# Context's post norm, next norm, keys and values beside the latents' network, and weight splits first in the context's steps

## What is computed

```python
for i in range(DEPTH):                      # DEPTH = 2
    sh1, sc1, gt1, sh2, sc2, gt2 = ada_mods(c, w_ada[i], b_ada[i])
    csh1, csc1, cgt1, csh2, csc2, cgt2 = ada_mods(c_ctx, w_ada[i], b_ada[i])
    h_lat = modulate(rms_norm(x, g_mix_pre[i]), sh1, sc1)
    h_ctx = modulate(rms_norm(ctx, g_mix_pre[i]), csh1, csc1)
    # i = 0: y = pool_mixer(h);  i = 1: y_lat = attention of x over keys of ctx and x
    x = x + gt1 * rms_norm(y_lat, g_mix_post[i])
    m_lat = sq_relu_mlp(modulate(rms_norm(x, g_mlp_pre[i]), sh2, sc2), w_mlp_in[i], w_mlp_out[i])
    x = x + gt2 * rms_norm(m_lat, g_mlp_post[i])
    if i == 0:                              # the same for ctx, with csh, csc, cgt
        ctx = ctx + cgt2 * rms_norm(m_ctx, g_mlp_post[i])
```

## Time and profile before

| | before |
|---|---|
| median of 3 runs | 3835.47 us (3830.47 to 3838.3) |
| profiled execution | 3837.7 us |
| its span | 3835.9 us |
| PE busy | 3651.2 us, 95% |
| DVE busy | 2173.2 us, 57% |
| ACT busy | 1311.9 us, 34% |
| POOL busy | 268.9 us, 7% |

### The profile page before, as it was taken

The page is one execution under the profiler, slowest core; times in us unless marked ns, Lnnn a source line. Parts: engine busy times, 40 slices in busy tenths (PEclk is TensorE's granted clock), DMA queues, the critical chain, the costliest instruction groups (busy, mean ns, idle before and its releaser), DMA issues.

```text
span 3835.9 us, 45608 instructions
## 1 busy us (share of the span) xinstructions
PE 3651.2 (95%) x18034; PEld 2952.3 (77%) x18034; DVE 2173.2 (57%) x3522; ACT 1311.9 (34%) x1876; POOL 268.9 (7%) x362
## 2 busy tenths in 40 slices
PE   6999999999999999999999999998899968999997
PEld 5888956788888888964789878888688746587886
DVE  6555544646545555644676768766655555544444
ACT  3222443233222322344224323444322235533221
POOL 0000122001000000113001010020000010200000
PEclk9999999999999999989999999999999968999998
DMA  5444201334442443310343343334333311012220
GB/s 230 180 159 161 101 23 53 135 129 166 163 165 110 170 165 139 122 71 1 107 176 121 136 161 148 137 122 165 121 147 134 137 50 44 1 45 88 99 98 34
DMA packets 84228, 451.94 MB, mean 118 GB/s; under 512 B 10192, under 2 KB 10640, under 8 KB 47152
## 3 DMA queue, kind: packets, MB, share of 16 engines
q1 hardware_dynamic: 81936, 439.35, 31.0%
q0 software_dynamic: 2080, 9.67, 0.7%
HBM read 446.88 MB, written 2.10 MB: 117 GB/s over the span
## 4 chain that ended last, share of the span: by engine, by line
PE 87%; DVE 5%; issue 3%; ACT 3%; POOL 1%; DMA 0%; DVEq 0%; SPq 0%; POOLq 0%; ACTq 0%
PE ps L607 22%; PE ps L606 22%; PE ps L608 22%; PE ps L1486 3%; PE ps L1522 2%; PE ps L2781 1%; PE ps L980 1%; PE ps L982 1%; PE ps L1504 1%; PE ps L981 1%; PE ps L1226 1%; PE ps L2195 1%; ACT WH L513 1%; PE ps L2196 1%; PE ps L2197 1%
## 5 line engine op out<-in xcount | busy, mean ns | idle before, releaser
L606 PE MATMUL ps<-nH,WH 128*128 128x512 f32 x2416 | 955.1, 395 | 7.1 <-DVE nL L738 7.1
L607 PE MATMUL ps<-nL,WH 128*128 128x512 f32 x2416 | 951.9, 394 | 0.0
L608 PE MATMUL ps<-nH,WL 128*128 128x512 f32 x2416 | 951.1, 394 | 0.0
L524 DVE TENSOR_TENSOR WL<-raw,WH 128x2048 fp32r<-128x2048 f32 (+2 forms) x308 | 673.6, 2191 | 483.2 <-ACT WH L513 482.3
L513 ACT ACTIVATE WH<-raw 128x2048 fp32r<-128x2048 f32 (+2 forms) x308 | 560.4, 1824 | 619.0 <-PE ps L608 579.2
L606 PEld LDWEIGHTS ps<-nH,WH 128*128 128x128 f32 x2416 | 457.3, 189 | 118.2 <-ACT nH L722 9.4
L607 PEld LDWEIGHTS ps<-nL,WH 128*128 128x128 f32 x2416 | 457.1, 189 | 101.7 <-issue 2.2
L608 PEld LDWEIGHTS ps<-nH,WL 128*128 128x128 f32 x2416 | 456.8, 189 | 98.4
L606 PE MATMUL ps<-hH,WH 128*128 128x512 f32 x1072 | 422.5, 394 | 2.2 <-DVE h L1193 2.2
L607 PE MATMUL ps<-hL,WH 128*128 128x512 f32 x1072 | 423.2, 395 | 0.0
L608 PE MATMUL ps<-hH,WL 128*128 128x512 f32 x1072 | 422.2, 394 | 0.0
(11 more groups left out here) (395 smaller groups left out, 5344.0 us busy)
## 6 DMA issues: line engine op xcount, KB each, us to landing
raw<-in_wst SPq DMA_DIRECT2D x282, 1024.0 KB, 4.8
araw<-in_ast SPq DMA_DIRECT2D x225, 512.0 KB, 5.7
raw<-in_wst SPq DMA_DIRECT2D x18, 512.0 KB, 3.4
row<-in_ast SPq DMA_DIRECT2D x15, 512.0 KB, 15.0
cw<-in_cw POOLq DMA_DIRECT2D x4, 1024.0 KB, 6.0
h<-in_xT SPq DMA_DIRECT2D x1, 2048.0 KB, 8.4
raw<-in_wst SPq DMA_DIRECT2D x8, 256.0 KB, 2.6
out<-h SPq DMA_DIRECT2D x8, 256.0 KB, 2.0
```

The source lines that it names most:

```text
L524: dve.q.tensor_tensor(M.WL[k % NW][:, 0:n], M.raw[k % NR][:, 0:n], M.WH[k % NW][:, 0:n].bitcast(F32), ALU.subtract).then_inc(*v_wlo.up(k))
L606: pe.q.matmul(to, hi[:, i, cc], xh, start=i == 0, stop=False)
L607: pe.q.matmul(to, hi[:, i, cc], xl, start=False, stop=False)
L608: t = pe.q.matmul(to, lo[:, i, cc], xh, start=False, stop=i == nk - 1)
```

## The change

- In `context_on_act` and `context_on_dve` the `yield` moves: a step does the weight split, then lets the latents' step run, and only then its own hidden layer.
- `latents_*` has 31 steps instead of 34. The sum of the first norms comes at step 3, the pools at 10, 12, 14, 16; DVE applies the pooling mean one step ahead of ACT's `gH`, and `scr` is used with four tiles instead of two where the input of the pool is made.
- The context's post norm leaves `context_on_*`. Together with the next norm, keys and values it forms `tail_*`, which runs step by step beside the latents' network from its first step. The key's two weight slots stand in the plan behind the network's seventeenth and eighteenth.
- Modulation rows: two instead of one in every other slot of the latents' network, none in the key's slots.
- The context's keys and the latents' keys go to `cB`, which must wait for the last modulation row; scratch tiles move; `narrow`, which takes two of the eight banks away, comes behind the projections of the attention; a wait of the `ma` copies for the context is dropped.

```diff
-POOLED_STEPS = (11, 13, 15, 17)
-RENEWED = {22: (0, 1), 23: (2,), 24: (3, 4), 25: (5,), 26: (6, 7)}
-LATENTS_STEPS = 34
+POOLED_STEPS = (10, 12, 14, 16)
+RENEWED = {19: (0, 1), 20: (2,), 21: (3, 4), 22: (5,), 23: (6, 7)}
+LATENTS_STEPS = 31
+
+KEYS_STEP = 16
...
-    cols("w_qkv_2", (0,), 0, KT, 1024, 512, 256)
+    for n in range(2):
+        out.insert(SHARED[1] + KEYS_STEP + 1 + 2 * n, ("w_qkv_2", (0,), 0, KT, 1024 + 256 * n, 256))
...
+        if a[:5] == "w_mlp" and k % 2 == 0:
+            more = 2
...
-        if SHARED[0] <= k < SHARED[1]:
+        if SHARED[0] <= k < SHARED[1] or a == "w_qkv_2":
...
+    key.scr = [M.cB[1][:, i * C:i * C + C] for i in range(4)]
+    key.qx, key.ssq = key.scr[1:3], (key.scr[0], key.scr[3])
+    key.rs = key.small
+    key.srs = key.small[:, :].rearrange("p (a b) -> p a b", a=2)
...
-            lat.vT = sb(sc, "vT", [128, S])
+            lat.vT = [sb(sc, f"vT{i}", [128, S]) for i in range(2)]
...
-        def mlp2_dve(dve, g, p, l, q, was, free):
-
-            into = into_ma(p, M.ma)(g)
-
-            def sink(dve, ci, o):
-                if ci == 0:
-                    dve.wait_ge(*free(o))
-                into(dve, ci, o)
-
-            yield from ffn_dve(dve, g, p, NF2, False, M.hH2, M.hL2, sink)
+        def mlp2_dve(dve, g, p, l, q, was):
+            yield from ffn_dve(dve, g, p, NF2, False, M.hH2, M.hL2, into_ma(p, M.ma)(g))
...
             for ci in range(CHUNKS2):
                 for f in (0, 2):
                     step_dve(dve)
+                    yield
                     hidden(ci, f)
-                    yield
                 for _ in range(2 if ci else 0):
                     step_dve(dve)
                     yield
             for _ in range(2):
                 step_dve(dve)
                 yield
-            yield from post_dve(dve, g + "post", con, lambda i: M.mac[:, i, :], lambda i: a_ev.to(g, "acc", i // 2),
-                                V("g_mlp_post_2", 0), mod(2, 0, 5, 1), v_mod.to(2, 0, 5, 1), x_after(con, "ctxpoolpost"))
...
+        FIRST = ((0, 1, 2), (3, 4), (5, 6), (7,))
+
         def latents_pe(pe):
             for s in range(LATENTS_STEPS):
-                if s == 4:
+                if s == 3:
                     b, free = take(FIN, "sum")
                     pe.wait_ge(*free)
                     pe.wait_ge(*v_ssum.to(FIN, 7))
@@ -2362,25 +2353,24 @@
                         pe.q.matmul(b[:, 4 + j:5 + j], M.fin[2][:, c], M.ones[:, 0:1], start=True, stop=False)
                         t = pe.q.matmul(b[:, 4 + j:5 + j], lat.scr[2][:, c], M.epsc[:, 0:1], start=False, stop=True)
                     t.then_inc(*mm.up(FIN, "sum"))
-                if s == 5:
+                if s == 4:
+                    spread_pe(pe, POOL2, M.fin[3])
...
-                if s == 20:
+                if s == 17:
                     sum_pe(pe, POST2, M.fin[2])
-                if s == 21:
+                if s == 18:
                     spread_pe(pe, POST2, lat.scr[3])
-                if s == 27:
+                if s == 24:
                     put_back(POST2, "rstd")
-                if s == 28:
                     sum_pe(pe, MLP2, M.fin[2])
-                if s == 29:
+                if s == 25:
...
-                if s in (6, 7):
+                if s in (5, 6):
                     dve.wait_ge(*mm.to(POOL2, "rstd"))
-                    for i in range(4 * s - 24, 4 * s - 20):
-                        if i >= 2:
-                            dve.wait_ge(*a_xhi.to(POOL2, i - 2))
+                    dve.wait_ge(*mm.to(FIN, "rstd"))
+                    for i in range(4 * s - 20, 4 * s - 16):
+                        if i >= 4:
+                            dve.wait_ge(*a_xhi.to(POOL2, i - 4))
                         ev = empties(v_xr, POOL2, "rstd") if i == 7 else v_xr.up(POOL2, i)
-                        dve.q.tensor_tensor(lat.scr[i % 2][:, :], h_tile(i), bank(POOL2, "rstd")[:, :], ALU.mult).then_inc(*ev)
+                        dve.q.tensor_tensor(lat.scr[i % 4][:, :], h_tile(i), bank(POOL2, "rstd")[:, :], ALU.mult).then_inc(*ev)
                         if i == 7:
                             v_xr.again(POOL2, 7)
-                if 8 <= s < 16:
-                    f = s - 8
+                if 7 <= s < 15:
+                    f = s - 7
...
+                                  v_ylo.to(POOL2, f - 2) if f >= 2 else a_xhi.to(POOL2, 4 + f))
+                if 8 <= s < 16:
+                    pool_low_dve(dve, POOL2, s - 8, M.gH, M.gL, lat.scr[s % 2][:, :])
+                if s - 1 in POOLED_STEPS:
+                    for i in (s - 11, s - 10):
                         add(POST2, i, M.fin[2], odd)
-                if s == 20:
+                if s == 18:
                     inverse(POST2)
...
-                if s >= 30:
+                if 26 <= s < 30:
                     dve.wait_ge(*mm.to(MLP2, "rstd"))
-                    for i in (2 * s - 60, 2 * s - 59):
+                    for i in (2 * s - 52, 2 * s - 51):
                         times2_dve(dve, i)
-                        if i:
-                            low2_dve(dve, i - 1)
-                if s == LATENTS_STEPS - 1:
+                        if i >= 2:
+                            low2_dve(dve, i - 2)
+                if s == 30:
+                    low2_dve(dve, 6)
...
+        def tail_pe(pe):
             g, p = "ctxkey", key
+            yield from norm_pe(pe, "ctxmlppost", p)
             yield from norm_pe(pe, g, p)
             xs, ready = normed_x(p, g)
             slot_pair(pe, "w_qkv_2", C, xs, ready, [("kc0", "raw"), ("kc1", "raw")])
             yield
             slot_pair(pe, "w_qkv_2", C, xs, ready, [(g, "v", i) for i in range(2)])
-            values_pe(pe, g, p)
             yield
             for name in ("kc0", "kc1"):
                 head_pe(pe, p, name)
+            yield
+            values_pe(pe, g, p)
+            yield
+            yield
             for name in ("kc0", "kc1"):
                 head_spread_pe(pe, p, name)
...
+        def tail_dve(dve):
             g, p = "ctxkey", key
+            yield from post_dve(dve, "ctxmlppost", p, lambda i: M.mac[:, i, :], lambda i: a_ev.to("ctxmlp", "acc", i // 2),
+                                V("g_mlp_post_2", 0), mod(2, 0, 5, 1), v_mod.to(2, 0, 5, 1), x_after(con, "ctxpoolpost"))
             gain_dve(dve, g, V("g_mix_pre_2", 8), 2, 1, 0, 1)
-            dve.wait_ge(*mm.to("latmlp0", "o", last_chunk(NF2), 7))
             yield from norm_dve(dve, g, p, x_tile(con), x_after(con, "ctxmlppost"), ())
             step_dve(dve)
             yield
             step_dve(dve)
+            yield
+            yield
+            yield
             values_dve(dve, g, p, 0)
-            yield
             for name in ("kc0", "kc1"):
                 head_root_dve(dve, p, name)
+            yield
+            yield
+            dve.wait_ge(*v_row.to(8 * len(adas) - 1))
             for i, name in enumerate(("kc0", "kc1")):
                 head_out_dve(dve, p, name, key_dst(p, i), False)
...
-            now.extra = narrow()
-            weave(latents_on_pe(pe), keys_pe(pe), beside_latents)
+            weave(latents_on_pe(pe), tail_pe(pe), beside_context)
```

More of the change, by code:

```diff
@@ L332, in memory @@
             M.hL2 = sb(sc, "hL2", [128, 2, 4, S], F32R)
[L333 to L344, removed]
-    cx.close()
+            key.small = sb(sc, "smallk", [128, 16])
+            with ExitStack() as one:
+                M.mac = sb(one, "mac", [128, KT, C])
+            with ExitStack() as one:
+                key.nH = sb(one, "nHk", [128, KT, C], F32R)
+    kv = ExitStack()
+    M.Vtk = sb(kv, "Vtk", [128, 6, 256], side="right")
+    cx.close()
+    with ExitStack() as ph:
+        key.nL = sb(ph, "nLk", [128, KT, C], F32R)
+    with ExitStack() as ph:
+        key.sdg, key.vT = ([sb(ph, f"{n}k{i}", [128, C]) for i in range(2)] for n in ("sdg", "vT"))
+    key.scr = [M.cB[1][:, i * C:i * C + C] for i in range(4)]
+    key.qx, key.ssq = key.scr[1:3], (key.scr[0], key.scr[3])
+    key.rs = key.small
+    key.srs = key.small[:, :].rearrange("p (a b) -> p a b", a=2)
     with ExitStack() as ph:
@@ L2268, in context_on_act @@
                 yield
-            for j in range(4):
-                act.wait_ge(*mm.to(g, "acc", j))
-                act.q.activation(M.mac[:, 2 * j:2 * j + 2, :],
-                                 bank(g, "acc", j)[:, :].rearrange("p (a b) -> p a b", a=2), ACT.Copy
-                                 ).then_inc(*empties(a_ev, g, "acc", j))
-            yield from post_act(act, g + "post", con, lambda i: M.mac[:, i, :], lambda i: a_ev.to(g, "acc", i // 2), ())
         def context_on_dve(dve):
@@ L2421, in latents_act @@
                         act.wait_ge(*v_xr.to(POOL2, i))
-                        act.q.activation(M.hp[:, i, 8:S + 8], lat.scr[i % 2][:, :], ACT.Identity, scale=both[:, i:i + 1],
```

(20 more changed lines are left out.)

66 lines of the change are left out of this document (27 added, 39 removed).

## The result

The change took 3809.77 us in the median of 6 runs (3797.93 to 3817.07), against 3836.22 of before (also 6 runs): a ratio of 0.9934, with a 95% interval of 0.9913 to 0.9955. It is faster by 26.5 us, where 46 were forecast. The profiled execution of the change was the lowest of its six (span 3796.1 us).

A forecast was written before the change was run, and what follows sets the result against it. PE's waits and lower clock outside the full latents' network were taken as the only room for gain. Terms of -22, -17.7, +18.5 and -24.8 made -46 us: 3790 us, range 3774 to 3812.

The forecast's parts named there:

- Term 1: Context's steps: fewer PE waits and less time at a low clock, -22 us; bounds nothing to 38 us.
- I take half of the 17 us: Context's steps: fewer long idle pieces win back half of the 17 us that the lower clock took.
- The second of the prediction's signs of being wrong: Context's steps: ACT still waits some 30 us for DVE's `scr`.
- Term 2: Behind the context's network: the norm's stretch with PE idle goes, -17.7 us.
- Term 3: Latents' network: moved matmuls, sums and transposes add PE time, plus 3 us of waits, +18.5 us.
- rival (d): Latents' network: PE meets the keys' slot before the last `nLk`, waits up to 10 us, clock falls; 3800 us.
- The bound of +68: Latents' network: upper bound in us if all 21 steps with rows took 13.5 us.
- Term 4: Behind the latents' network: only a post norm and a norm left, 38.1 us instead of 62.9, -24.8 us.
- case (a): Context's steps: little won, as POOL's window sums slow DVE; 3797.5 us, or 3811.5 with lower clock; chance 0.14.
- (b): Latents' network: doubled modulation rows make DVE the bound; 3839 us and above; chance 0.05 for above 3815.
- the likeliest case: Whole kernel: the forecast together with rival (d), 3778 to 3803 us, chance 0.72.

The follow-up runs named there:

- the run with 34: Kernel with both remedies, its last three latents' steps two steps later, two of them behind the context's last slot; 3793.3 us (0.9902).
- both remedies: Changed kernel with first sum at step 4 (32 steps) and, from step 18, latents' step ahead of the weight split; 3790.4 and 3789.4 us.

## Why the prediction was right and where it failed

**Term 1 failed: -22 us forecast, -2.6 measured.** The step that failed is the sum "The waits become 3.9 (`nLc`, unchanged) + 2 + 5 = 11 instead of 25 us." Its 2 us for `gL`, the third pool and the sum in `cB` measured 5.0 (2.5 + 0 + 2.5), its 5 us for the first sum 5.3, and the second sum, which it put at nothing, 7.0: 19.4 us in all with `nLc` (2.1). I walked through the first sum as the shorter plan has it. I did not do this for the other two, though the diff moves them as well. Before, each sum stands one step behind its last additions: additions at 3, 19 and 27, sums at 4, 20 and 28. In the change additions and sum share a step: 3, 17 and 24. So the chain from ACT's square to DVE's last addition lies on PE's path three times, 14.8 us instead of the 5 in the forecast. Splits first makes it longer at the second sum, because a copy that waits for its load stands ahead of the eviction. The runs bear this out from both sides: a step more, or the latents ahead of the split, takes the 7.0 us to 1.3 or 2.0, and a step more at the first sum takes the 5.3 to 0.2.

The distance in steps is not all of it. The third sum waited 11.6 us before, and 8.2 with only the yield moved, with a step between; in the change, with none, 2.5. Before, ACT squares the new `h` in the step in which DVE makes it, and waits for it (in the context's steps, us in total, times, longest):

```profile
ACT fin L2392 <- DVE h L2519: 6.2, 2, 4.0
...
ACT cB L2392 <- DVE h L2519: 4.6, 2, 3.8
```

In the change ACT's squares come one step later, and it waits for no `h`. That this is what the third sum gained by is likely, but no run tries it alone.

**The clock gave nothing back.** "I take half of the 17 us" was a gain of 8.5 us. PE was busy for 218.2 us where before it was 214.9, at 0.92 instead of 0.93; the same steps in the run with all rows doubled had 216.0 at 0.94, so some of this is scatter. Of what term 1 missed, 8.5 us are waits (11 forecast, 19.4 measured) and some 12 are this (its parts make 23 us, which the forecast took as 22). The waits are fewer in us than before (19.4 against 25.3), in four places of over 2 us instead of three; why the busy time did not fall with them stays open. It falls once the sums are mended (207.1 us at 0.98), and the stretch is then 214.9 and 216.9 us, the low end of the 215 to 220 that the forecast gave the change.

**The reason given for the gain was not the reason.** The prediction took DVE's 57.7 and ACT's 33.0 us of waits for the loss. With the yield alone ACT's 33.0 stay (32.4) and 12.5 us are won. In the change they are gone, as the forecast had it, and in the run with the yield put back they are 1.0 while the stretch is 8.2 us longer than before; what the mean a step ahead is worth by itself was not tried. What the yield does is only partly shown: the waits at the pools (8.9 to 6.3) and at the third sum (11.6 to 8.2) come down with it. That this comes from DVE reaching the latents' work 1.4 us earlier in every other step is argued.

The second of the prediction's signs of being wrong, ACT still waiting some 30 us for `scr`, could not have shown this failure. The length of the context's steps and PE's largest wait did: 237.6 us instead of 215 to 220, and 7.0 us at the second sum instead of 5 at the first.

**Term 2 was right** (-17.7 us; no idle time is left there), but the plan of 31 steps was not needed for it: the run with 34 has none either. What is left as its source is that the post norm went from this place. So the shorter plan cost 8 to 10 us in the context's steps and bought next to nothing behind them. A plan of before's 34 steps with the tail beside the network was not tried.

**Term 3 was right in size** (+18.5, measured +19.4). Its wait of 3 us came as 3.3, at another place than rival (d) had it: PE meets the key's slot without a wait, and waits for a bank in the slot behind it, because DVE does a second row, after 5.07 us of waiting for it, ahead of the additions into `ma`. Eleven waits of about 5 us for the rows were forecast; they measured 5.2. (The bound of +68 is 67 by its own numbers, 15.5 + 21 x 2.44, which changes nothing.)

**Term 4 was right** (-24.8, measured -25.0): the chain of a post norm and a norm, put together from pieces of the last stages, holds to 0.2 us (37.9 against 38.1).

**The rivals.** By its numbers the result is case (a): 3803 to 3815, term 1 going towards nothing. Its mechanism was there, but is not what made PE wait. Groups of DVE's instructions in the context's steps (count, busy us, mean ns), first the change, then the kernel before with only the yield moved:

```profile
L2279 DVE TENSOR_TENSOR hLc<-mid,hHc 128x512 fp32r<-128x512 f32 x16 | 13.0, 814 | 0.6
...
L2444 DVE TENSOR_TENSOR cB<-cB 128x512 f32<-128x512 f32 x6 | 5.0, 841 | 0.4
...
L2276 DVE TENSOR_TENSOR mid<-mid 128x512 f32<-128x512 f32 x16 | 12.7, 793 | 8.6 <-ACT mid L2248 8.6
...
L2444 DVE TENSOR_TENSOR cB<-cB,fin 128x512 f32<-128x512 f32 x12 | 9.1, 758 | 0.1
```

```profile
L2285 DVE TENSOR_TENSOR mid<-mid 128x512 f32<-128x512 f32 x16 | 13.9, 866 | 8.0 <-ACT mid L2251 8.0
```

`hLc` was at 692 ns before and is at 814, `mid` at 684 and is at 793, the additions into `cB` at 690 and 684 and are at 841 and 758, while `gL` has 1342 in both: more of DVE's instructions meet POOL's window sums, as the rule of the Trainium skill (SBUF — State Buffer, section Who interferes with whom) has it. That is 5.5 us of DVE's time, near the 8 us that (a) prices. But the kernel with only the yield moved has much the same (`mid` at 866, `hLc` at 739, 3.7 us for the two) and is 12.5 us shorter than before, and the one with both remedies has 4.3 us in these four groups and a stretch of 216.9. So this is not what held PE in the change. (b) is real and one notch away: with every other slot doubled 3.3 us reach PE, with all of them 29. The range, 3774 to 3812, held the time only near its upper end, through a case (a) that came about for another reason, which is luck; the likeliest case's own, to 3803, did not.

## What to carry to other kernels

When a plan by steps is shortened, list for every reduction the steps of its last producer and of its consumer, before and after; a distance of nought puts an ACT and DVE chain on the engine that consumes, however idle the others look. A step between is no proof of the contrary: look at what ACT and DVE have ahead of the last addition in their own order, as at the third sum here. On an in-order queue ask what the instruction ahead of the urgent one waits for: a copy that waits for its load holds back an eviction that is ready. And take an engine's total of waits (33 us of ACT for `scr`) for its own idle time until a wait of the bounding engine is seen to follow from it.

## What the runs showed of the hardware

- Fewer waits of PE mostly came with less busy time for the same matmuls, but at no fixed rate. In the context's steps, waits, busy time and granted clock were 25.3 us, 214.9 us and 0.93 before; 17.0, 210.7 and 0.96 with only the yield moved; 19.4, 218.2 and 0.92 in the change, and 22.1, 216.0 and 0.94 for the same steps in the run with all rows doubled; 9.8, 207.1 and 0.98 with both remedies.
- An addition into `cB` of 128x512, both inputs in SBUF, took 0.69 us at 2580.48 in the change's trace, and 1.54 and 1.60 us at 2551.09 and 2552.74, while POOL's window sums ran.
